# Attention stage of a two-layer diffusion backbone: where the softmax denominators are made, and when TensorE turns the rows of maxima

## The reference, cut to what matters

```python
MLA_HEADS = 8; QK_HEAD = 96; V_HEAD = 64; SEQ = 2048; CTX_LEN = 256

def attend_context(q, k, v):                      # 256 context queries, 256 keys
    s = jnp.einsum('bqhe,bkhe->bhqk', q, k).astype(jnp.float32) * (QK_HEAD ** -0.5)
    p = jax.nn.softmax(s, axis=-1).astype(v.dtype)
    return jnp.einsum('bhqk,bkhd->bqhd', p, v).reshape(b, t, h * V_HEAD)

def attend_latent(q, k_lat, v_lat, k_ctx, v_ctx): # 2048 latent queries, 2304 keys
    ...
        s = jnp.concatenate([jnp.einsum('bqhe,bhke->bhqk', qi, kl),
                             jnp.einsum('bqhe,bhke->bhqk', qi, kc)], axis=-1)
        p = jax.nn.softmax(s.astype(jnp.float32) * (QK_HEAD ** -0.5), axis=-1).astype(vl.dtype)
        return (jnp.einsum('bhqk,bhkd->bhqd', p[..., :n], vl)
                + jnp.einsum('bhqk,bhkd->bhqd', p[..., n:], vc))
```

## Time and profile before

| | |
|---|---|
| time, median of 3 runs | 4982.51 us (4974.69 to 4991.34) |
| the profiled execution | 4986.26 us, of which its span is 4984.3 us |
| attention stage, from its first turn to its last output | 829 to 1938 us of the span |
| TensorE busy over the span | 4627.2 us, 93% |
| VectorE, ScalarE, GpSimd busy | 2674.8, 1794.7, 1380.7 us |
| granted TensorE clock, mean | 0.968 of 2.4 GHz |

### The profile page before, as it was taken

The page is one execution under the profiler, slowest core; times in us unless marked ns, Lnnn a source line. Parts: engine busy times, 40 slices in busy tenths (PEclk is TensorE's granted clock), DMA queues, the critical chain, the costliest instruction groups (busy, mean ns, idle before and its releaser), DMA issues. The chain is left out here.

```text
span 4984.3 us, 120707 instructions
## 1 busy us (share of the span) xinstructions
PE 4627.2 (93%) x48510; PEld 2745.2 (55%) x48510; DVE 2674.8 (54%) x4780; ACT 1794.7 (36%) x4413; POOL 1380.7 (28%) x2884
## 2 busy tenths in 40 slices
PE   6999996999999999899999997999998989999599
PEld 3666663333333333454444445787777778778544
DVE  2444443655666663232144336666666667666476
ACT  1222221444344443033122223555555545555332
POOL 1111111332322331000000002455555455555343
PEclk8999997999999999899999998999999999999799
DMA  5222223000000002632321235666666666666575
GB/s 215 93 86 97 85 77 127 4 25 23 25 24 24 25 6 102 223 135 102 116 76 58 69 94 169 169 181 170 177 167 174 165 165 177 174 178 172 150 228 177
DMA packets 938529, 585.99 MB, mean 118 GB/s; under 512 B 659125, under 2 KB 882997, under 8 KB 923960
## 3 DMA queue, kind: packets, MB, share of 16 engines
q1 hardware_dynamic: 851514, 556.33, 37.7%
q10 hardware_dynamic: 86528, 22.82, 2.1%
HBM read 382.11 MB, written 196.88 MB: 116 GB/s over the span
## 5 line engine op out<-in xcount | busy, mean ns | idle before, releaser
L934 PE MATMUL at_bS<-at_qT,at_kT 97*64 97x512 f32 (+1 forms) x2368 | 607.5, 599 | 15.1 <-ACT at_pT L1032 14.5
L1645 PE MATMUL p_bU<-keep_hT,p_slab 128*128 128x512 f32 (+1 forms) x1504 | 591.3, 554 | 12.7 <-DMA p_slab<-in_o_w_in_dram 7.3
L1069 DVE TENSOR_REDUCE at_mx<-at_bM 128x1 f32<-128x512 f32 (+1 forms) x656 | 394.1, 627 | 354.0 <-PE at_bM L899 353.1
L2267 PE MATMUL rw_bank<-keep_rw_hg,rw_slab 128*128 128x256 f32 x2048 | 478.5, 387 | 8.8 <-DMA keep_rw_hg<-scratch_hT 8.7
L1032 ACT ACTIVATE at_pT<-at_bS 128x512 f32<-128x512 f32 (+1 forms) x592 | 342.4, 591 | 398.3 <-PE at_bS L934 378.9
L1645 PEld LDWEIGHTS p_bU<-keep_hT,p_slab 128*128 128x128 f32 x1504 | 286.6, 191 | 311.0 <-issue 282.7
L2267 PEld LDWEIGHTS rw_bank<-keep_rw_hg,rw_slab 128*128 128x128 f32 x2048 | 380.1, 190 | 72.4 <-issue 11.6
L856 POOL TENSOR_TENSOR at_sum_pool<-at_sum_pool,at_pT 128x512 f32<-128x512 f32 x192 | 243.9, 1270 | 372.3 <-ACT at_pT L1032 354.9
L2051 POOL TENSOR_TENSOR rw_g_at<-rw_g_at,rw_g_prod 64x14 f32<-64x14 f32 (+6 forms) x1008 | 321.3, 319 | 78.9
L2049 POOL TENSOR_TENSOR rw_g_prod<-rw_g_at 64x14 f32<-64x14 f32 (+6 forms) x1008 | 311.3, 309 | 79.1
L934 PEld LDWEIGHTS at_bS<-at_qT,at_kT 97*64 97x64 f32 x2368 | 155.5, 137 | 279.7 <-issue 187.5
(11 more groups left out here) (288 smaller groups left out, 9658.6 us busy)
## 6 DMA issues: line engine op xcount, KB each, us to landing
keep_wide<-scratch_heads SPq DMA_DIRECT2D x144, 512.0 KB, 6.9
keep_rw_hg<-scratch_hT SPq DMA_DIRECT2D x64, 1024.0 KB, 6.8
keep_gate<-scratch_inverses SPq DMA_DIRECT2D x576, 64.0 KB
scratch_bv<-keep_wide SPq DMA_DIRECT2D x144, 128.0 KB, 5.4
scratch_products<-rw_NB SPq DMA_DIRECT2D x288, 64.0 KB
scratch_y<-rw_ysb ACTq DMA_DIRECT2D x288, 64.0 KB, 3.0
scratch_heads<-p_z SPq DMA_DIRECT2D x17, 1024.0 KB, 4.9
m_yin<-scratch_y SPq DMA_DIRECT2D x32, 512.0 KB, 5.6
```

What stands on the lines that cost most here:

```text
L934: last = pe.matmul(bS[rows, g % 3, 0:nq * P], kT[:, s, k * P + VH * x:k * P + VH * x + VH], qT[:, s, q0 * P:(q0 + nq) * P], start=True, st ...
L1069: nc.vector.tensor_reduce(mx[:, j, piece:piece + 1], bM[:, (FIRST_ITEM[b] + i) % 2, 0:n], AX.X, ALU.max).then_inc(max_red, 1)
L1645: last = pe.matmul(bU[:, n % 4, 0:w], slab[:, i, k, :], hT[:, k, tok:tok + w], start=(k == 0), stop=(k == KD - 1))
L2267: last = pe.matmul(DENSE[:, GT * half:GT * (half + 1)], slab[:, half, q, :], hg[:, x.slot, q, :], start=(q == 0 and half == 0), stop=(q == ...
```

## The change

The row of ones no longer stands still while the sums are streamed: each [128 x 128] piece of `sumD` becomes the stationary operand and one column `ones` is streamed, which gives the denominators of 128 queries as a column on 128 partitions. It is written to column 64 of the piece's place in `bR`, where `finish` read it before. The copy by ScalarE, the wait of `o_transposes` for it and row 64 of `oT` go away; the output turns write 64 columns instead of 65. Second, a `row` that comes due within a pair (other than a block's last pair) is kept back and issued after that pair's values.

```diff
-        oT = core.sb("oT", [VH + 1, 2, 512])
+        oT = core.sb("oT", [VH, 2, 512])
...
                 def denominators(h, s, b, rows_done):
-                    n, count = BLOCKS[b][1] * P, h * NBLK + b
+                    count = h * NBLK + b
                     pe.wait_ge(added[False], h * ADDS[False] + adds_of["end", b][False])
                     pe.wait_ge(row_out, rows_done)
                     pe.wait_ge(o_done, count)
-                    pe.matmul(bR[0:1, 0:n], ones[:], sumD[:, (s + b) % 2, 0:n], start=True, stop=True).then_inc(den_mm, 1)
+                    for j in range(BLOCKS[b][1]):
+                        last = pe.matmul(bR[:, j * P + VH:j * P + VH + 1], sumD[:, (s + b) % 2, j * P:(j + 1) * P], ones[:], start=True, stop=True)
+                    last.then_inc(den_mm, 1)
 
                 def o_transposes(h, s, b):
                     pe.wait_ge(oT_out, h * NBLK + b + 1)
-                    pe.wait_ge(den_out, h * NBLK + b + 1)
                     for j in range(BLOCKS[b][1]):
-                        last = pe.transpose(bR[:, j * P:j * P + VH + 1], oT[:, (s + b) % 2, j * P:(j + 1) * P], ident[0:VH + 1, 0:VH + 1])
+                        last = pe.transpose(bR[:, j * P:j * P + VH], oT[:, (s + b) % 2, j * P:(j + 1) * P], ident[0:VH, 0:VH])
                     last.then_inc(o_tr, 1)
...
+                            rows_due = []
                             for k in (2 * pair, 2 * pair + 1):
                                 if k + 2 < nk:
                                     scores(h, s, b, k + 2)
                                 for kind, hh, ss, n, i in jobs[k]:
                                     if kind == "max":
                                         max_item(hh, ss, n, i)
+                                    elif kind == "row" and pair < nk // 2 - 1:
+                                        rows_due.append((hh, ss, n))
                                     elif kind == "row":
                                         row(hh, ss, n, h * NBLK + b)
...
                             pv(h, s, b, pair, has_next)
+                            for hh, ss, n in rows_due:
+                                row(hh, ss, n, h * NBLK + b)
...
-                def denominators_out(h, s, b):
-                    n, count = BLOCKS[b][1] * P, h * NBLK + b
-                    if not (isinstance(count, int) and count < 2):
-                        a.wait_ge(o_tr, count - 1)
-                    a.wait_ge(den_mm, count + 1)
-                    nc.scalar.copy(oT[VH:VH + 1, (s + b) % 2, 0:n], bR[0:1, 0:n]).then_inc(den_out, 1)
```

More of the change, by code:

```diff
@@ L706, in attend @@
         added, odd_out = {False: sem("at_added_vector"), True: sem("at_added_pool")}, sem("at_odd_out")
-        den_mm, den_out = sem("at_denominators"), sem("at_denominators_out")
+        den_mm = sem("at_denominators")
         settled = [sem(f"at_settled{i}") for i in range(2)]
@@ L1035, in head @@
                     for b in range(NBLK):
-                        jobs, due = beside(b, s, h, has_next), outputs(h, s, b, has_before)
+                        jobs = beside(b, s, h, has_next)
                         nk = STEPS[b]
@@ L1045, in head @@
                                     row(hh, ss, bb)
[L1046 to L1049, removed]
                         for kind, hh, ss, bb, i in jobs[nk - 1]:
@@ L1058, in _ @@
                 heads(head)
-                for b in (3, 4):
-                    denominators_out(HEADS - 1, 1, b)
             @block.vector
```

## The result

The changed kernel takes 5014.34 us, median of 4 runs (5012.28 to 5019.64), against 4985.35 for the kernel before (4 runs): ratio 1.0066, 95% interval 1.005 to 1.0081. That is 29 us slower; the forecast was +16.8 and a range up to 5012. The profiled execution has a span of 5010.5 us, 26.2 longer than before.

The account below looks back on a forecast made before the run. TensorE was taken to set the pace, busy 1038.5 of 1070 us in attention's heads. The terms +1.8 - 0.9 + 16.8 - 0.9 gave +16.8 us, so 4982.5 became 4999.3 us, range 4986 to 5012.

Parts of the forecast that it names:

- Part 1: Denominators on TensorE: 1.14 us a block instead of 1.09, +1.8 us over the attention stage.
- L229 rows: First-stage rows of the same load-and-one-column form, taken as price model: 0.112 us per load with its column.
- Part 2: ScalarE's denominators copy removed: 0 inside the heads, -0.9 us at the attention stage's end.
- Part 3: Rows issued behind the values, leaving ScalarE's copy uncovered: +16.8 us at normal places, -0.9 us at late rows.
- 24 normal places: Places where the moved row waits for nothing late: +0.70 us each, +16.8 us in all.
- The sign named: If right, about 31 waits of scores for ScalarE's copy into `qT`, 0.7 us each, 20 us or more.
- The late rows: The 7 rows for block 1 in heads 1 to 7, waiting for old outputs: -0.13 us each, -0.9 us.
- rival (b): Copy's way partly covered or paid back, four head-turn clock falls vanish (-7 us): about 4992 us; chance 0.24.
- (a): Clock falls at the 24 new gaps: 5010 us if every fourth falls, +41 if all; chance 0.18.
- the last part: Signs of a right forecast, among them the attention stage 17 us longer and nothing else changed.

Follow-up runs that it names:

- rows only: The kernel before with only the rows of maxima moved behind the values, denominators as before: 4997.24 us, ratio 1.0024.
- changed + 136: The changed kernel with 34 idle one-column matmuls at attention's opening, its list 512 instructions longer than before: 4997.16 us, ratio 1.0019.
- the three with late rows only: Kernel before, only 7 head-turn rows kept back: 4979.97 us; plus 48 idle matmuls: 4985.55; instead plus the changed kernel's denominators and 34 idle matmuls: 4982.91.

## Why the prediction was wrong

**Part 1 was right.** Forecast 1.14 us for a block's denominators against 1.09; measured +0.03 from denominators to scores, so about +1.1 over the stage where +1.8 stood. The L229 rows were the right model. The Trainium skill's price of 81 ns a pair at N = 128 (TensorE: Matmul & The Clock Gate, "Back-to-back issue gap") doesn't fit here: eight pairs last 1.05 with their drain of 0.25, so 0.80 for seven intervals, 0.11 each.

**Part 2 was right**: there is no change of the waits for exponentials (14.5 to 14.2 us), and from the last values to the stage's end it is 5.1 us where 6.0 was, the -0.9 forecast.

**Part 3 was right in size.** 0.66 of standing for the copy, 1.26 us from turn to scores, as worked out. The count of 24 normal places was right, but not their kind: 17 wait at the scores, 7 at the values of block 3, and that these 7 cost nearly the same is luck. The sign named, 31 waits for the copy and 20 us or more, came out as 25 and 16.6. The late rows gave 0.17 each, not 0.13. With the rows alone attention took 8.8 us more with four falls gone, so 8.8 + 6.7 = 15.5 without that; forecast 16.8 - 0.9 = 15.9.

**The clock** went the way of rival (b), not (a). The standing time at head turns was split in two, 0.81 and 0.66. Behind none of the 42 turns in the six kernels of this form did the clock fall (changed, rows only, changed + 136, and the three with late rows only); in the six with the old form it fell behind 22 of 42. Whether the split or the shorter sum kept the clock up stays open. Nor did it fall behind any of the 24 new gaps. The prediction's sum had held the falls as they were; -6.7 belongs there. By the measured terms attention is 1.1 + 15.5 - 6.7 - 0.9 = 9.0, less 0.6 for the clock's earlier rise at the start, so 8.4; the stage measured 7.9.

**What failed** is a sentence in how the bound was read, "a microsecond more or less in TensorE's list is one in the result", and in the last part "nothing else changed". Part 1 priced the 416 added and 40 removed instructions by their time where they stand, and not by what they do to the list behind them. +19.3 us came there: not by more instructions, but because 376 isn't a multiple of 256. The measured result is thus rival (b)'s 4992 plus some 20 us that no rival had. Luck could have hidden both errors: with the list 512 instructions longer the kernel took 4997.16 us, inside the range and near the 4999.3 forecast, though attention took 8 us more and not 17. It can't be told from the trace of before what a shift of 120 costs; that long waits stand at one position of each 256 could have been.

**Open.** Why position 242 has more long waits than 106 is open. The stage's rows repeat, so a border may fall again and again on a fast stretch, but borders behind less than 3.2 us are about as many in the two traces (55 before, 57 changed); a wait stands at 27 of the first and at 40 of the second. The part of the other transfers is open too: the DMA share is 0.66 in the recurrent stage and 0.08 in attention, where no such wait over 0.4 us was seen, but attention also takes its instructions more slowly, 10 matmuls and loads a microsecond against 43. No run changed either alone. The stage also varies by 11 us between profiles at one position (1682.0 to 1693.0), which is unexplained.

## What to carry to other kernels

Before an operation is moved behind another, ask what the next instruction in the list waits for: a row that must pass through ScalarE needs about 0.7 us of other work behind it, and keeping back only the 7 rows that really came late won 8 us of attention where keeping back all lost 9, though the total doesn't show it beyond its interval. When a stage that wasn't touched changes its time, number the engine's instructions and look at where its waits without a releaser stand, modulo the 256 of a fetched piece; a few idle instructions early on can test it, and here could undo it. A shorter and split wait can save more by the clock (6.7 us here) than by its own length (1.2).

## What the runs showed of the hardware

- TensorE's instructions come in packets of 16384 bytes, one for each 256 instructions, and each of the 664 long waits without a releaser in the twelve profiles' recurrent stages (0.4 to 3.5 us) ends 2.2 to 3.4 us after such a packet started and stands at one position modulo 256 that moves with the length of the list, to within 2. The Trainium skill (Runtime: NRT & Kernel Launch, "Instruction fetch mechanics") gives blocks of that size and says that crossing a border is mostly hidden. The trace agrees on the size; hidden it is not in this stage: 43 waits, 61.6 us of 1682.9 at the best position, 69 and 91.0 at the worst seen.
- The clock fell behind 22 of 42 head turns with one gap of 1.67 us of standing, and behind none of 42 with two of 0.81 and 0.66 and four turning matmuls between. Without streaming it was 2.4 us in the first form (scores 1159.41 and their 0.86, to values at 1162.64) and 2.2 in the second (values 1160.61 and their 0.86, to scores at 1163.70). The Trainium skill says that turns don't count as a busy TensorE in the way matmuls do (TensorE: Matmul & The Clock Gate, "Part 4: PE-mode transpose"). These runs neither show nor refute it: the standing fell from 1.67 to 1.47 in all and the stretch without streaming from 2.4 to 2.2, so the sums got shorter as well as split, and no run held either still.
- A load of 128 x 128 float32 with one streamed column costs 0.11 us in a row of them, so turning a float32 product round, from 512 streamed columns to four pieces of two such loads, changes 0.95 to 0.98 us.
